# Low parts of seven weight tiles moved from VectorE to GpSimd, and kernel products of two pairs on two column tiles, in a two-layer diffusion backbone

## What is computed

```
ql, kl, vl, gl, ul = jnp.split(h_lat @ w_in, cuts, axis=-1)
...
lam_bar = jnp.exp(lam * dt)
b_bar = ((lam_bar - 1.0) / lam)[..., None] * lax.complex(b_re[direction], b_im[direction])
...
bu_l = jnp.einsum('gpk,blgk->blgp', b_bar, order(ul).astype(jnp.complex64))
x_l = ssm_scan(lam_bar, bu_l)
ys_l = ys_l + order(jnp.einsum('gkp,blgp->blgk', c_mat, x_l).real)
```

## Time and profile before

| | |
|---|---|
| time, median of 3 runs | 1870.78 us (1870.18 to 1872.35) |
| time of the profiled execution | 1870.6 us |
| its span, first to last instruction | 1868.8 us |
| TensorE busy | 1793.0 us, 96% |
| VectorE busy | 1194.6 us, 64% |
| ScalarE busy | 747.0 us, 40% |
| GpSimd busy | 61.7 us, 3% |
| mean granted TensorE clock | 0.979 of full speed |

### The profile page before, as it was taken

How to read it: one execution, slowest core, us unless ns; L and a number is a source line. 1 busy time by engine, 2 the same in 40 slices (tenths; PEclk the granted TensorE clock), 3 DMA queues, 4 the chain that set the end, 5 groups by cost and what they waited for, 6 DMA issues and landing times.

```text
span 1868.8 us, 25130 instructions
## 1 busy us (share of the span) xinstructions
PE 1793.0 (96%) x9640; PEld 1516.5 (81%) x9640; DVE 1194.6 (64%) x1846; ACT 747.0 (40%) x1054; POOL 61.7 (3%) x41
## 2 busy tenths in 40 slices
PE   7999999999888898999999999999999999989998
PEld 5788888877787687888888878888888797789997
DVE  4677677788999745776676367766333434855554
ACT  4422222346888625221232343222222533754343
POOL 0000000020000020000000200000002000010001
PEclk9999999999999998999999989999999899989999
DMA  8554455331101132644553335454223241034543
GB/s 328 183 206 157 174 194 200 109 111 68 46 35 35 46 113 91 223 147 169 202 203 114 112 146 191 146 181 168 90 78 118 107 170 68 10 127 174 186 171 122
DMA packets 40436, 257.74 MB, mean 138 GB/s; under 512 B 4752, under 2 KB 6032, under 8 KB 15536
## 3 DMA queue, kind: packets, MB, share of 16 engines
q1 hardware_dynamic: 40368, 256.86, 37.8%
HBM read 255.79 MB, written 1.05 MB: 137 GB/s over the span
## 4 chain that ended last, share of the span: by engine, by line
PE 85%; DVE 9%; ACT 4%; issue 2%; DMA 1%; DVEq 0%; SPq 0%; ACTq 0%
PE ps_all L1638 26%; PE ps_all L1642 26%; PE ps_all L1639 26%; DVE w_lo L975 2%; PE banks L1690 1%; ACT w_hi L541 1%; DVE sq_acc L1369 1%; PE ps_all L1634 1%; PE banks L2098 1%; PE banks L1912 1%; PE banks L1763 1%; PE ps_all L2075 1%; DVE normed L1378 0%; DVE wb L1333 0%; DVE scaled L1360 0%
## 5 line engine op out<-in xcount | busy, mean ns | idle before, releaser
L1638 PE MATMUL ps_all<-a_hi,w_lo 128*128 128x512 f32 (+1 forms) x1768 | 648.6, 367 | 16.4 <-ACT a_hi L638 9.7
L1642 PE MATMUL ps_all<-a_lo,w_hi 128*128 128x512 f32 (+1 forms) x1768 | 643.3, 364 | 0.2 <-DVE a_lo L1113 0.2
L1639 PE MATMUL ps_all<-a_hi,w_hi 128*128 128x512 f32 (+1 forms) x1768 | 642.6, 363 | 0.0
L975 DVE TENSOR_TENSOR w_lo<-w_raw,w_hi 128x2048 fp32r<-128x2048 f32 (+3 forms) x183 | 374.2, 2045 | 157.4 <-ACT w_hi L541 157.2
L541 ACT ACTIVATE w_hi<-w_raw 128x2048 fp32r<-128x2048 f32 (+3 forms) x183 | 313.5, 1713 | 327.3 <-PE ps_all L1642 317.9
L1638 PEld LDWEIGHTS ps_all<-a_hi,w_lo 128*128 128x128 f32 x1768 | 338.2, 191 | 72.7 <-issue 11.7
L1642 PEld LDWEIGHTS ps_all<-a_lo,w_hi 128*128 128x128 f32 x1768 | 337.9, 191 | 54.5 <-DVE a_lo L1113 3.4
L1639 PEld LDWEIGHTS ps_all<-a_hi,w_hi 128*128 128x128 f32 x1768 | 338.7, 192 | 50.5 <-issue 0.2
L987 DVE SCALAR_TENSOR_TENSOR mod_junk<-mod_raw,cond 128x1024 bf16<-128x1024 f32 x256 | 302.7, 1219 | 7.7 <-ACT cond L569 5.4
L1638 PE MATMUL ps_all<-g_hi,w_lo 128*128 128x512 f32 (+1 forms) x704 | 257.6, 366 | 1.9 <-DVE w_lo L975 1.9
L1642 PE MATMUL ps_all<-g_lo,w_hi 128*128 128x512 f32 (+1 forms) x704 | 256.1, 364 | 0.0
(11 more groups left out here) (254 smaller groups left out, 1499.4 us busy)
## 6 DMA issues: line engine op xcount, KB each, us to landing
w_raw<-in_tiles SPq DMA_DIRECT2D x118, 1024.0 KB, 4.8
mod_raw<-in_w_mod SPq DMA_DIRECT2D x64, 1024.0 KB, 4.8
w_raw<-in_tiles SPq DMA_DIRECT2D x32, 768.0 KB, 4.1
w_raw<-in_tiles SPq DMA_DIRECT2D x32, 640.0 KB, 3.8
start_w<-in_w_start SPq DMA_DIRECT2D x8, 1024.0 KB, 19.7
bias<-in_na_bias SPq DMA_DIRECT2D x2, 1536.0 KB, 8.7
h<-in_h SPq DMA_DIRECT2D x4, 512.0 KB, 5.7
cond<-in_cond SPq DMA_DIRECT2D x2, 1024.0 KB, 18.1
```

The source lines that it names most:

```text
L975: nc.vector.tensor_tensor(w_lo[:, slot, 0:size], w_raw[:, slot, 0:size], w_hi[:, slot, 0:size].bitcast(F32), ALU.subtract).then_inc(lo_rea ...
L1638: pe.matmul(dst, w[1], x[0], start=start, stop=False)
L1639: pe.matmul(dst, w[0], x[0], start=False, stop=False)
L1642: return pe.matmul(dst, w[0], x[1], start=False, stop=stop_)
```

## The change

The subtraction for tiles 1 to 8 of the loop goes to GpSimd, which waits on `hi_ready` and counts a new semaphore `low`. VectorE no longer subtracts there. It waits on `low` in `low_made`, at the end of a turn, writes one column of a small tile `told`, and with that write counts `lo_ready`, so that the order of this semaphore stays as it was. The kernel products of two pairs are issued together and alternate between two column tiles: one pair writes partitions 0 to 31 of `ps_sum`, the other partitions 32 to 63, both in columns 0 to 223. `kernel_rows` reads them from there.

```diff
@@ ScalarE, kernel_rows
                     for s in range(4):
-                        at = 224 * ql + 32 * (3 - s)
-                        ins = nc.scalar.activation(kt[32 * s:32 * s + 32, b % 2, ql, :], ps_sum[0:32, at:at + P], ACT.Copy)
+                        at = 32 * (3 - s)
+                        ins = nc.scalar.activation(kt[32 * s:32 * s + 32, b % 2, ql, :],
+                                                   ps_sum[32 * ql:32 * ql + 32, at:at + P], ACT.Copy)
@@ VectorE, mixer0
+                def low_made(j):
+
+                    dve.wait_ge(S["low"], j)
+                    nc.vector.memset(told[:, j - 1:j], 0.0).then_inc(lo_ready, 1)
+
                 dve.wait_ge(S["pads"], 1)
                 build_w(0)
                 fraction(0)
                 build_c(0)
-                split_lo(base + 1, 2048, 1)
+                low_made(1)
                 for b in range(8):
                     rotate(2 * b)
                     turn_back(2 * b)
                     if b < 7:
                         build_w(b + 1)
-                    if b < 7:
-                        split_lo(base + b + 2, 2048 if b < 6 else width("glu"), b % 2)
                     rotate(2 * b + 1)
                     turn_back(2 * b + 1)
...
                     if b < 4:
                         rope(b)
+                    if b < 7:
+                        low_made(b + 2)
@@ GpSimd, mixer0
+                for j in range(1, 9):
+                    n, size, slot = BASE["ret_in"] + j, 2048 if j < 8 else width("glu"), j % 2
+                    pool.wait_ge(hi_ready, n + 1)
+                    nc.gpsimd.tensor_tensor(w_lo[:, slot, 0:size], w_raw[:, slot, 0:size],
+                                            w_hi[:, slot, 0:size].bitcast(F32), ALU.subtract).then_inc(S["low"], 1)
@@ TensorE, kernel_products(b) in place of kernel_products(pair)
-                    for ri in range(2):
-                        pe.matmul(ps_sum[0:32, at:at + 96], bwd[ri], state_rows(c[ri][:, 6:9]), start=(ri == 0), stop=(ri == 1))
-                    pe.matmul(ps_sum[0:32, at + 96:at + 224], fwd[0], state_rows(c[0][:, 0:4]), start=True, stop=False)
-                    pe.matmul(ps_sum[0:32, at + 96:at + 224], fwd[1], state_rows(c[1][:, 0:4]), start=False, stop=False)
+                    to = [ps_sum[32 * ql:32 * ql + 32] for ql in range(2)]
                     for ri in range(2):
-                        pe.matmul(ps_sum[0:32, at + 96:at + 128], bwd[ri], c[ri][:, 9, :], start=False, stop=False)
+                        for ql in range(2):
+                            pe.matmul(to[ql][:, 0:96], bwd[ql][ri], state_rows(c[ql][ri][:, 6:9]), start=(ri == 0), stop=(ri == 1))
+                    for ri in range(2):
+                        for ql in range(2):
+                            pe.matmul(to[ql][:, 96:224], fwd[ql][ri], state_rows(c[ql][ri][:, 0:4]), start=(ri == 0), stop=False)
...
```

More of the change, by code:

```diff
@@ L206, in program @@
         warm = sbuf("warm", [P, 1])
+        told = sbuf("told", [P, 8])
         std = sbuf("std", [P, 4])
@@ L329, in program @@
             "ang", "magic", "frac", "abs", "tables", "turned", "vt", "v", "kmm", "k", "rot", "z", "rates", "scan",
-            "back", "x", "y", "gelu")}
+            "back", "x", "y", "gelu", "low")}
         ret_sem = {n: sem("ret_" + n) for n in (
@@ L1846, in inputs_to_state, with kernel_products @@
                     mm.then_inc(S["v"], 1)
-                def kernel_products(pair):
-                    b, ql = pair // 2, pair % 2
-                    at = 224 * ql
+                def kernel_products(b):
                     pe.wait_ge(S["c"], b + 1)
@@ L1855, in kernel_products @@
                         pe.wait_ge(S["k"], 2 * b)
-                    c = [cp[:, b % 2, ql, ri] for ri in range(2)]
-                    fwd = [wb[:, 2 * ql, ri, 3, :] for ri in range(2)]
-                    bwd = [wb[:, 2 * ql + 1, ri, 0, :] for ri in range(2)]
+                    c = [[cp[:, b % 2, ql, ri] for ri in range(2)] for ql in range(2)]
+                    fwd = [[wb[:, 2 * ql, ri, 3, :] for ri in range(2)] for ql in range(2)]
+                    bwd = [[wb[:, 2 * ql + 1, ri, 0, :] for ri in range(2)] for ql in range(2)]
+                    to = [ps_sum[32 * ql:32 * ql + 32] for ql in range(2)]
                     for ri in range(2):
-                        pe.matmul(ps_sum[0:32, at:at + 96], bwd[ri], state_rows(c[ri][:, 6:9]), start=(ri == 0), stop=(ri == 1))
-                    pe.matmul(ps_sum[0:32, at + 96:at + 224], fwd[0], state_rows(c[0][:, 0:4]), start=True, stop=False)
-                    pe.matmul(ps_sum[0:32, at + 96:at + 224], fwd[1], state_rows(c[1][:, 0:4]), start=False, stop=False)
+                        for ql in range(2):
+                            pe.matmul(to[ql][:, 0:96], bwd[ql][ri], state_rows(c[ql][ri][:, 6:9]), start=(ri == 0), stop=(ri == 1))
                     for ri in range(2):
-                        pe.matmul(ps_sum[0:32, at + 96:at + 128], bwd[ri], c[ri][:, 9, :], start=False, stop=False)
-                    pe.matmul(ps_sum[0:32, at + 96:at + 128], const[0:32, C_IDENT:C_IDENT + 32], skip[:, pair, :],
-                              start=False, stop=True).then_inc(S["kmm"], 1)
+                        for ql in range(2):
+                            pe.matmul(to[ql][:, 96:224], fwd[ql][ri], state_rows(c[ql][ri][:, 0:4]), start=(ri == 0), stop=False)
+                    for ri in range(2):
+                        for ql in range(2):
+                            pe.matmul(to[ql][:, 96:128], bwd[ql][ri], c[ql][ri][:, 9, :], start=False, stop=False)
+                    for ql in range(2):
+                        pe.matmul(to[ql][:, 96:128], const[0:32, C_IDENT:C_IDENT + 32], skip[:, 2 * b + ql, :],
+                                  start=False, stop=True).then_inc(S["kmm"], 1)
                 def outputs(pair):
@@ L1891, in mixer0 @@
                 kernel_products(0)
-                kernel_products(1)
                 def head_scores(hd):
@@ L1982, in mixer0 @@
                     if b < 7:
-                        kernel_products(2 * b + 2)
-                        kernel_products(2 * b + 3)
+                        kernel_products(b + 1)
                 head_scores(1)
```

## The result

| | before | changed |
|---|---|---|
| time, median (lowest to highest) | 1870.56 us (1870.18 to 1872.35), 4 runs | 1884.51 us (1883.85 to 1885.60), 4 runs |
| ratio, 95% interval | | 1.0069, 1.0056 to 1.0082: slower |
| profiled execution, its span | 1870.6 us, 1868.8 us | 1884.1 us, 1882.2 us |
| mean granted TensorE clock | 0.979 | 0.971 |

The change costs 14 us, 0.7%. The first thing to look at is GpSimd's own order of time in the loop of the changed kernel, since its rows are new. Each row gives start, duration, engine, line and operation; in brackets how long the engine had waited and for what. (The change moves eight low parts, seven of 2048 columns and one of 1024.)

What follows compares the result with a forecast made beforehand. VectorE was taken to bound the state-space loop. Tile 1 +1.15, tiles 2 to 6 +11.2, tile 7 +0.9, tile 8 +1.1 and `told` +0.6 made +15.0 us on 1870.6, forecast 1885.5 us, range 1876 to 1892 us.

Steps and rivals of the forecast that it cites:

- the working of tile 1: Before the loop: GpSimd's subtraction holds VectorE during `prod`, so the first `rotate` starts at 450.75, not 449.63; +1.15 us.
- VectorE sets this stage: State-space loop, 447 to 600 us: a microsecond on VectorE is one of the kernel; the other engines' time is covered.
- The hold, 4.45 us for 2048 columns: GpSimd's subtraction shuts out VectorE operations with two SBUF inputs: 4.45 us for 2048 columns, 2.25 for 1024.
- The line through 256 and 512 columns: Estimate from GpSimd sums in the trace: holds of 0.60 and 1.15 us, so 0.55 us for each further 256 columns.
- Where it falls: In the loop's turns GpSimd's hold meets VectorE's four `wb` sums, with nothing beside it, the same turn after turn.
- The rival in which the hold slips: The hold comes behind the `wb` sums; L1360 and L1361 hide 1.3 us in all turns: +7.2, 1878 us; 17%.
- this turn at +2.24: Tiles 2 to 6, turns b = 0 to 4: hold 4.45 less 2.21 us saved on VectorE, +2.24 each, +11.2 together.
- Tile 7, +0.9: Turn b = 5: VectorE runs two PSUM-reading operations of `rotate` beside the hold, 1.3 us; the rest costs +0.9 us.
- Tile 8, +1.1: Turn b = 6, 1024 columns: the hold of 2.25 us falls inside the `wb` sums, less 1.15 saved; +1.1 us.
- `told`, +0.6: VectorE's one-column write and its wait: 0.15 us, exposed in the four turns with a `rope`; +0.6 us.
- Column tiles, 0: TensorE's kernel products save 0 to 1.2 us a turn, but wait for VectorE's `cp`; costed at 0.
- Falls of the clock: TensorE idles before the `wb` transposes and its clock falls; no cost expected; if exposed in six turns, +14, 1899 us; 7%.

Runs made afterwards that it cites:

- the halves: Against the changed kernel, VectorE subtracts the second half of each tile itself and GpSimd only the first half; 1880.92 us, ratio 1.0040 to the kernel before.

## Why the prediction was right

Forecast 1885.5 us, measured 1884.51: the order of the events was as told but for one turn, and the terms stand so. Two slips of arithmetic are in the sum: the working of tile 1 gives 450.75 − 449.63 = 1.12 and not 1.15, and the 0.2 us by which the profiled execution lies under the median should have been added to 1885.6, not taken off, which makes 1885.8. Neither matters at this size.

- **VectorE sets this stage.** Right. In all nine experiments the turns of tiles 4 to 6 grew and shrank by what VectorE's chain lost or saved. It has a limit: without a hold VectorE waits for others elsewhere (3.39 us for TensorE ahead of tile 2, 0.63 and 0.83 for `tcos` later), and the turns of tiles 3 and 8 are only 1.5 and 0.4 us shorter, where 2.2 and 1.15 were taken off VectorE.
- **The hold, 4.45 us for 2048 columns.** Right: 4.40 at tile 1 and 4.43 at tile 4 (4.24 at tile 6). The line through 256 and 512 columns carried to 2048 within 0.05 us at most tiles. For 1024 it gave 2.25; measured 2.12 at tile 8 (3.84 − 1.72) and 2.20 in the halves. The Trainium skill's 4.497 us (GPSIMD Engine Reference, "Elementwise — side-by-side cycle accounting") lies between the hold and the raw rows of 4.67, which have VectorE's running instruction in them.
- **Where it falls.** Right for tiles 1 (on `prod`), 4, 5, 6 and 8 (on `wb`) and 7 (on L1365); tile 2's fell on `prod`, which costs the same. Wrong for tile 3: "the place stays the same turn after turn" held only while ScalarE had no other delay. The rival in which the hold slips came true in this one turn, by the second of the ways it named, a later high part (1.5 us later). What made it late no term had: the hold made `wb` late, TensorE, quicker by its column tiles, waited, its clock fell, and the transposes and so ScalarE were late. It gave back 1.5 us, and the forecast had this turn at +2.24 where +0.75 was measured.
- **Tile 7, +0.9.** Measured +1.50. The slipped hold itself was as told: L1365 stands until 584.4, and the forecast's way of counting gives 579.80 + 4.45 = 584.25. The other 0.5 us is the same lateness of ScalarE, here at a cost: VectorE waited 0.69 us for `tcos` at 570.92, where it had waited 0.23 before. No term of the sum had this.
- **Tile 8, +1.1.** Measured +0.99.
- **`told`, +0.6.** Wrong, it costs nothing. The write takes 0.06 us, and L1362 behind `rope` starts as early as it did, 475.92 − 469.73 = 6.19 us behind `tsin` against 6.18:

```profile
475.92 0.69 DVE L1362 TENSOR_TENSOR scaled<-banks,tcos 128x512 f32<-128x512 f32 x1
475.94 0.06 DVE L1401 MEMSET told<- 128x1 f32 x1
```

- **Column tiles, 0.** Right alone: 0.9995. Two pairs start at 521.48 and are done at about 522.75 at a clock of 1.00, 1.3 us against 2.36; it was saved and waited away. Together with the hold they were not quite nothing: the longer wait that they leave TensorE stands ahead of the fall of the clock and the slip at tile 3, 1.4 us by two traces.
- **Falls of the clock: to be expected and without cost.** They came, at 0.50 and 0.64 in the rows above. In the loop they had no cost of their own, only the two effects on ScalarE, −1.5 and +0.5. Behind the loop a fall cost some 3 us, and later stages gave about that back; I had put nothing there.

The sum forecast was +15.0, the turns show +12.94, and the profiled execution +13.5: +0.7 ahead of the loop, +12.9 in it, +3.4 in the stretch behind, −3.6 later. The mechanism and the hold were right. That the total came within 1 us is in part luck: inside the loop the terms are 2.1 us too high together (tile 3 −1.5, `told` −0.6, tile 7 +0.6 and smaller ones), 0.7 us came in ahead of it, where the two programs are alike, and the loss and the gain behind it happen to cancel.

## What to carry to other kernels

Before work goes to an idle GpSimd, look at what the bounding VectorE does at that moment. Beside VectorE instructions with two SBUF inputs the subtraction cost its whole time on GpSimd (4.4 us to save 2.2), counted by the hold and not by its raw row; beside instructions that read PSUM it was free up to the cover that the rows show (1.3 us, 512 columns). A saving on an engine that waits for the bounding one is worth nothing, and when the bounding engine gets slower, look one and two engines further: here its lateness came back to it through TensorE and ScalarE.

## What the runs showed of the hardware

- A GpSimd instruction that only writes (a clearing of 2048 columns, 1.82 us) runs beside VectorE's two-input sums with no delay to either.
- The hold goes by columns and hardly by instructions: 1.02 us for 512 columns in a row of four, 2.20 for 1024, 4.40 for 2048. GpSimd's own rows beside the PSUM readers read 1.27 for 512 and 2.36 for 1024.
- A wait of TensorE for a held `wb` can be followed by a lower granted clock: 2.57 us, and then 0.50 from 465.5 to 467.5 us; after a wait of 1.33 us at the same place of another kernel it stayed at 1.00.
